# PEER feed-forward of a decode step: the seventh token block's up rows are fetched and added on VectorE instead of being multiplied on TensorE

## The chip, the cores and the metric

One NeuronCore of a Trainium2 chip. The metric is the device time of one execution in microseconds (us). The program is written directly for the five engines with semaphores; each engine runs its own list of instructions in order.

## The reference, cut to what matters

One decoder layer (convolution, window attention, memory attention, PEER feed-forward) for a prompt of 1024 tokens and 8 sample tokens, model width 1024, all in float32. The change touches only the last part, the PEER feed-forward:

```
q = (xb @ w_q).reshape(PEER_BLOCK, PEER_HEADS, 2, PEER_DK_HALF)
s = jnp.einsum('thcd,hcnd->thcn', q, keys, preferred_element_type=jnp.float32)
sv, si = lax.top_k(s, PEER_TOPK)
...
eid = i0 * PEER_N_KEYS + i1
gate = jax.nn.softmax(cv, axis=-1)
u = w_down[eid]
act = jax.nn.gelu(jnp.einsum('td,thkd->thk', xb, u, preferred_element_type=jnp.float32), approximate=False)
return jnp.einsum('thk,thkd->td', (gate * act).astype(xb.dtype), w_up[eid])
```

Every token selects 8 heads x 16 = 128 experts of 16384. For each it needs one row of `w_down` (1024 floats) for a dot product and one row of `w_up`, scaled by gate times activation, for the sum. The output is x1 plus this sum, followed by a final RMS norm.

## The kernel before, in words

The prompt is cut in 8 blocks of 128 tokens (one token on each partition). Attention and the projections run first; from about 1100 us on, the PEER part bounds the work, in three streams.

**Down rows.** For slot j of block n, GpSimd issues one indirect DMA that gathers 128 rows of `w_down`, one for each token: 512 KB (L1404, `fetch`). VectorE multiplies them with x and sums (L2019, `dot(n, j)`): 8 x 128 = 1024 such dots. Before them VectorE picks the experts (`keys`, `ids`). The rows land in a ring of SBUF slots (`rows_at`); GpSimd may fetch into a slot again once VectorE has used it. Six or seven slots are in use in the late part; one more holds the block's own x.

**Dense up.** For blocks 0 to 6 the up product is not gathered: the 128 coefficients of a token are scattered to a 128 x 128 x 128 table (VectorE builds one-hot vectors, L2043, `hot`; ScalarE scales them, L2321; TensorE multiplies them, L1469, `scatter`; ScalarE copies the table out, L2355), and TensorE multiplies this table with the whole of `w_up`. `w_up` is 128 pieces of 512 KB (L1275, `fetch_up`, on SyncE's queue, a ring of 4). The blocks are staggered by half a table: in pass n (64 pieces) TensorE multiplies each piece for block n-1 and for block n (L1666, `up_step`). So passes 0 and 7 have one block at each step ("single steps"), passes 1 to 6 two ("double steps"); passes 0 to 7 fetch 8 x 64 = 512 pieces. In the second half of pass n the table of block n+1 is scattered, one scatter at each step. When pass m+1 is over, VectorE adds block m's product to x1 (L2051, `sum`), ScalarE squares it, VectorE norms it (L2059, `norm`), SyncE writes it.

**Gathered up.** For block 7 GpSimd gathers 128 rows of `w_up` with the same ids, again 512 KB each, after the last down row, and VectorE adds each, scaled by its coefficient, to an accumulator (L2113, `up`). The adds depend on one another, so there is one semaphore wait between two.

**Sample tokens.** The 8 sample tokens' lists are made on the way. GpSimd gathers their 8 transfers of down rows (`sdown`, L1421; GpSimd first waits for the lists, which ScalarE writes and reads back after the squares of a sum), SyncE fetches 8 copies of their x rows (`scratch_xn`), VectorE makes the dots (`sdot`), GpSimd gathers 8 transfers of up rows (`sup`, L1427), TensorE sums them in the last pass ahead of step 56 (L1696), VectorE adds (`ssum`, L2095) and norms (`snorm`).

**What sets the order.** A planner (`Model`) walks through a modelled time at build and writes one list, `plan`; each engine takes its share of that list in order. So a `sum` or `ssum` stands at a fixed place among VectorE's dots, whatever the chip's real timing is: if what it waits for comes late, the dots behind it wait too.

## Time and profile before

| | us |
|---|---|
| three runs | 3344.72, 3355.07, 3366.14 |
| median of the runs | 3355.07 |
| span of the profiled execution | 3347.1 |
| busy in it: TensorE, VectorE, GpSimd | 3087.0, 2512.8, 1611.7 |
| moved by DMA in it | 1077.16 MB, 322 GB/s over the span |

The span reaches from the first to the last instruction of the profiled execution; its own time outside of the profiler is not listed, so the span stands 8.0 us under the median of the three runs. "Busy" is summed over instructions. The DMA share is the mean busy share of the 16 DMA engines; GB/s is what they moved. A "transfer" is called here what moves 512 KB (524288 bytes): one gathered row for 128 tokens, or one piece of `w_up`.

### The profile page before, as it was taken

Reading aid. Unit: us, or ns where it says so; the run is one execution under the profiler, and the core shown is the slowest. Engines: PE = TensorE matmul, PEld = TensorE weight load, DVE = VectorE, ACT = ScalarE, POOL = GpSimd, SP = SyncE. Lnnn points to the kernel's source line nnn. Section 1 sums busy time; section 2 is a strip of 40 time slices with the busy share of each in tenths; the row PEclk is TensorE's granted clock in tenths of the full one; section 3 lists DMA queues with packets and bytes.
Section 4 is the critical chain, followed back from the end, with each engine's and each line's share of the span. In section 5 each row is a group of like instructions: output and inputs, shape, how many; then the busy total and the mean of one; then the engine's idle time right before and its main releaser. Section 6 shows DMA issues by size and latency. Waiting matters only on the chain.

```text
span 3347.1 us, 33154 instructions
## 1 busy us (share of the span) xinstructions
PE 3087.0 (92%) x11349; PEld 1818.7 (54%) x11349; DVE 2512.8 (75%) x5082; ACT 779.2 (23%) x2063; POOL 1611.7 (48%) x1269
## 2 busy tenths in 40 slices
PE   8999798998989999779999999999999999997874
PEld 5677687866847654445545445545545545543321
DVE  2298434986889789888988888888888868455556
ACT  2001542321310114324214204204204214200000
POOL 0000002545145677745566667557657657444434
PEclk9999899999998999899999999999999999998998
DMA  3111466999599999999999999999999999899998
GB/s 130 43 37 58 147 204 231 336 334 354 197 339 351 359 404 397 331 368 370 381 353 388 357 380 388 344 389 385 358 377 380 359 400 373 335 410 393 408 410 316
DMA packets 326171, 1077.16 MB, mean 322 GB/s; under 512 B 40468, under 2 KB 73877, under 8 KB 325340
## 3 DMA queue, kind: packets, MB, share of 16 engines
q0 software_dynamic: 172416, 625.03, 48.7%
q1 hardware_dynamic: 119275, 428.87, 34.1%
q10 hardware_dynamic: 34312, 21.16, 2.0%
q8 instruction: 90, 1.47, 0.2%
q14 instruction: 78, 0.63, 0.1%
HBM read 1052.50 MB, written 23.94 MB: 322 GB/s over the span
## 4 chain that ended last, share of the span: by engine, by line
PE 29%; DMA 20%; DVE 15%; issue 13%; POOL 10%; ACT 1%; ACTq 1%; DVEq 0%; POOLq 0%
PE psum L1666 17%; DMA arena<-in_w_down,arena 12%; POOL arena L1404 9%; DMA arena<-in_w_up,arena 7%; DVE arena L2019 5%; PE psum L1469 4%; PE psum L1642 2%; PE psum L1529 2%; PE psum L1513 1%; ACTq L2264 1%; PE psum L1612 1%; DVE arena L2113 1%; DMA arena<-scratch_s 1%; DMA arena<-in_w_q 1%; PE psum L1515 1%
## 5 line engine op out<-in xcount | busy, mean ns | idle before, releaser
L1404 POOL DMA_INDIRECT arena<-in_w_down,arena x1024 | 1419.2, 1386 | 735.5 <-DVE arena L2019 503.1
L1666 PE MATMUL psum<-arena 128*128 128x512 f32 x3584 | 1602.0, 598 | 77.1 <-DMA arena<-in_w_up 70.8
L2019 DVE CUSTOM_DVE_ANT_0 arena<-arena 128x1024 f32<-128x1024 f32 x1024 | 1220.0, 1222 | 256.3 <-DMA arena<-in_w_down,arena 247.8
L1666 PEld LDWEIGHTS psum<-arena 128*128 128x128 f32 x3584 | 664.4, 191 | 871.0 <-issue 734.3
L1513 PE MATMUL psum<-arena 128*128 128x256 f32 (+2 forms) x1536 | 361.6, 390 | 17.0 <-DVEq L1831 5.5
L2321 ACT ACTIVATE arena<-arena 128x128 f32<-128x128 f32 x896 | 285.6, 390 | 323.8 <-DVE arena L2043 314.7
L2043 DVE TENSOR_TENSOR arena<-constants,arena 128x1024 f32<-128x1024 f32 x224 | 273.4, 1224 | 77.7 <-PE psum L1469 65.0
L1513 PEld LDWEIGHTS psum<-arena 128*128 128x128 f32 x1536 | 267.9, 195 | 99.5 <-issue 13.3
L1469 PEld LDWEIGHTS psum<-arena 128*128 128x128 f32 x1792 | 237.8, 195 | 153.2 <-ACT arena L2321 86.6
L1469 PE MATMUL psum<-arena 128*128 128x128 f32 x1792 | 245.0, 281 | 40.4 <-ACT arena L2321 40.2
L2113 DVE SCALAR_TENSOR_TENSOR arena<-arena 128x1024 f32<-128x1024 f32 x128 | 164.4, 1284 | 122.6 <-DMA arena<-in_w_up,arena 121.3
L1355 POOL DMA_DIRECT2D arena<-scratch_s x64 | 37.4, 585 | 423.5 <-DMA scratch_s<-arena 204.5
L284 PE MATMUL psum<-arena 128*128 128x344 f32 x816 | 238.4, 455 | 3.0 <-DVE arena L324 3.0
L1404 POOL DMA_INDIRECT arena<-in_w_up,arena x128 | 128.7, 1006 | 169.2 <-DVE arena L2113 150.1
L2355 ACT ACTIVATE arena<-psum 128x128 f32<-128x128 f32 (+5 forms) x512 | 149.4, 351 | 259.1 <-PE psum L1469 206.4
L284 PEld LDWEIGHTS psum<-arena 128*128 128x128 f32 x816 | 155.7, 191 | 85.3 <-issue 5.6
L1515 PE MATMUL psum<-arena 128*128 128x256 f32 (+2 forms) x768 | 183.2, 381 | 0.0
L1341 POOL MEMSET constants<- 128x64 f32 x1 | 0.2, 151 | 346.3 <-POOLq L369 346.3
L345 DVE SCALAR_TENSOR_TENSOR arena<-arena,constants 128x1024 f32<-128x1024 f32 x120 | 154.2, 1285 | 4.3
L1515 PEld LDWEIGHTS psum<-arena 128*128 128x128 f32 x768 | 132.8, 190 | 36.7
L1642 PE MATMUL psum<-arena 128*128 128x256 f32 (+2 forms) x512 | 126.1, 407 | 18.2 <-DMA arena<-in_w_q 11.3
L1529 PE MATMUL psum<-arena 128*128 128x512 f32 x256 | 119.8, 615 | 12.6 <-DVE constants L1824 5.8
(317 smaller groups left out, 2039.8 us busy)
## 6 DMA issues: line engine op xcount, KB each, us to landing
arena<-in_w_up SPq DMA_DIRECT2D x512, 512.0 KB
arena<-in_w_gates SPq DMA_DIRECT2D x96, 768.0 KB
arena<-in_w_o SPq DMA_DIRECT2D x40, 512.0 KB
arena<-in_w_q SPq DMA_DIRECT2D x32, 512.0 KB
arena<-in_w_down,arena POOLq DMA_INDIRECT x1024
arena<-in_w_chunks SPq DMA_DIRECT2D x26, 512.0 KB, 3.5
arena<-scratch_s POOLq DMA_DIRECT2D x64, 128.0 KB
scratch_s<-arena ACTq DMA_DIRECT2D x11, 512.0 KB
```

The lines of the kernel that those rows point to most:

```text
L284: mm = pe.matmul(psum[:, s + g, 0:GC], w[:, k, :], hT[:, k, g * GC:(g + 1) * GC], start=first, stop=last)
L1404: pool.indirect_dma_start(dst, None, table, bass.IndirectOffsetOnAxis(ap=idN[:, min(n, NT - 1) % 2, j:j + 1], axis=0)).then_inc(here, 16)
L1469: mm = pe.matmul(psum[:, 4 + g % 2, t * P:(t + 1) * P], pair[:, 1, t, :], pair[:, 0, t, :], start=True, stop=True)
L1513: pe.matmul(psum[:, b, 0:n], w[:, i, :], hT[:, i, cols], start=(i == 0), stop=(i == KD - 1))
L1515: mm = pe.matmul(psum[:, b + 1, 0:n], w[:, KD + c, :], branch[br][:, c, cols], start=(c == 0), stop=(c == NC - 1))
L1529: mm = pe.matmul(psum[0:tile_rows(t), bb + h, :], mergedT[:, t, i, :] if t < NT else mergedS[:, i, :], w[:, h * 512:(h + 1) * 512], start= ...
L1642: mm = pe.matmul(psum[:, b + h, 0:n], w[:, c, :], hT[:, c, cols], start=(c == 0), stop=(c == KD - 1))
L1666: mm = pe.matmul(psum[:, 2 * (m % 2) + h, :], coef_block(m, s % NKEYS), wup[s % WUPR][:, h * 512:(h + 1) * 512], start=first, stop=end)
L2019: dve.tensor_tensor_reduce(row, row, rowD[slot_of["x", n]], 1.0, 0.0, ALU.mult, ALU.add, dots[:, n % 3, j:j + 1]).then_inc(row_used, 1)
L2043: dve.tensor_tensor(hot_of(g), iota128.unsqueeze(1).unsqueeze(1).broadcast_to(full), ids[:, 0:2, BATCH * q:BATCH * (q + 1)].unsqueeze(3).b ...
L2113: dve.scalar_tensor_tensor(out=acc, in0=row, scalar=dots[:, (NT - 1) % 3, u:u + 1], in1=acc if u else x1last, op0=ALU.mult, op1=ALU.add).t ...
L2321: ins = act.activation(buf[:, 1, t, :], buf[:, 1, t, :], ACT.Copy, scale=ids[:, 2, c:c + 1])
```

## The change

`GB = 2` blocks, 6 and 7, now take the gathered way; `DENSE` falls from 7 to 6. The dense passes are 0 to 6 (pass 6 has single steps), so 64 pieces, one block's 32 scatters and one-hots, and 128 products of a piece with a table go away; 128 gathers of `w_up` rows and 128 adds come in. The ids of blocks 6 and 7 are both still held. Two accumulators stand where the one-hots were and take x1 by DMA; the slot of the last x is free for rows once its dots are over. Sample work is planned one pass earlier. The sum and norm of the last dense block no longer stand at the end of the plan but where the planner puts them.

```diff
-        DENSE = NT - 1
+        GB = 2
+        DENSE = NT - GB
...
-        for i in range(SLOTS * (NT + 1)):
+        for i in range(UPS):
...
-                free_from[s] = SLOTS * (f[1] + 1) if f[1] < NT - 1 else KEPT
+                free_from[s] = SLOTS * (f[1] + 1)
...
-        acc, x1last = at(40960, D), at(40960 + D, D)
-        y_at = [yb] * (DENSE - 1) + [rowD[slot_of["x", NT - 1]]]
-        rowS = [at(slot_at[5 if b < 4 else 7] + (b % 4) * D, D) for b in range(NB)]
-        xbc = [at(slot_at[0 if b < 4 else 2] + (b % 4) * D, D) for b in range(NB)]
-        ysm = at(slot_at[3], D)
+        accs = [at(40960 + D * i, D) for i in range(GB)]
+        rowS = [at(slot_at[2 if b < 4 else 3] + (b % 4) * D, D) for b in range(NB)]
+        xbc = [at(slot_at[4 if b < 4 else 6] + (b % 4) * D, D) for b in range(NB)]
+        ysm = at(slot_at[5], D)
...
-            if sum_next < DENSE - 1 and m.end.get(("passeded", sum_next + 1), m.now + 1) + (40.0 if sum_next == DENSE - 2 else 0.0) <= m.now:
+            if sum_next < DENSE and m.end.get(("passeded", sum_next + 1), m.now + 1) + (8.0 if sum_next == DENSE - 1 else 0.0) <= m.now:
...
-                    {"slist": (head_next % 2 == 0 or head_next // 2 % 2 == 1), "sdown": m.done("passeded", DENSE - 2), "ssum": last_put and m.done("suped", 0),
+                    {"slist": (head_next % 2 == 0 or head_next // 2 % 2 == 1), "sdown": m.done("passeded", DENSE - 2), "ssum": m.done("suped", 0),
...
-            if n_dot == NT and m.end.get(("passeded", DENSE - 2), m.now) + 20.0 > m.now:
+            if NT <= n_dot < NT + GB and (m.end.get(("passeded", DENSE - 2), m.now) + 20.0 > m.now or coefs <= n_dot - GB):
                 row = None
...
-        plan = m.plan + [(kind, DENSE - 1) for kind in ("sum", "norm")]
+        plan = m.plan
...
-                        table = w_down if n < NT else w_up
+                        table, u = (w_down, n) if n < NT else (w_up, n - GB)
                         pool.indirect_dma_start(dst, None, table, bass.IndirectOffsetOnAxis(
-                            ap=idN[:, min(n, NT - 1) % 2, j:j + 1], axis=0)).then_inc(here, 16)
+                            ap=idN[:, u % 2, j:j + 1], axis=0)).then_inc(here, 16)
...
                 def up(u):
-                    if u == 0:
-                        dve.wait_ge(coef_done, NT)
-                        dve.wait_ge(x1last_here, 16)
-                    else:
+                    g, j = u // SLOTS, u % SLOTS
+                    if j == 0:
+                        dve.wait_ge(coef_done, DENSE + g + 1)
+                        dve.wait_ge(x1last_here[g], 16)
+                    if u:
                         dve.wait_ge(up_sum, u)
                     row = row_wait(("up", u))
-                    dve.scalar_tensor_tensor(out=acc, in0=row, scalar=dots[:, (NT - 1) % 3, u:u + 1],
-                                             in1=acc if u else x1last, op0=ALU.mult, op1=ALU.add).then_inc(up_sum, 1)
+                    dve.scalar_tensor_tensor(out=accs[g], in0=row, scalar=dots[:, (DENSE + g) % 3, j:j + 1],
+                                             in1=accs[g], op0=ALU.mult, op1=ALU.add).then_inc(up_sum, 1)
```

The end of VectorE's list before. L2113 are the adds of up rows, L2118 and L2120 block 7's norm, L2095 to L2103 the sample tokens' sum and norm, L2051 to L2059 the sum and norm of block 6:

```order
L2113 SCALAR_TENSOR_TENSOR arena<-arena 128x1024 x31
L2051 TENSOR_TENSOR arena<-arena,psum 128x1024
...
L2113 SCALAR_TENSOR_TENSOR arena<-arena 128x1024 x81
L2118 RECIPROCAL constants<-constants 128x1
L2120 SCALAR_TENSOR_TENSOR arena<-arena,constants 128x1024
L2095 TENSOR_TENSOR arena<-arena,psum 8x1024
L2101 RECIPROCAL constants<-constants 8x1
L2103 SCALAR_TENSOR_TENSOR arena<-arena,constants 8x1024
L2051 TENSOR_TENSOR arena<-arena,psum 128x1024
L2057 RECIPROCAL constants<-constants 128x1
L2059 SCALAR_TENSOR_TENSOR arena<-arena,constants 128x1024
```

The same place now. The adds are L2119; L2029 makes block 7's coefficients; L2124 and L2126 norm a gathered block:

```order
L2024 ISA arena<-arena 128x1024
L2024 ISA arena 128x1
L2119 SCALAR_TENSOR_TENSOR arena<-arena 128x1024 x2
L2029 TENSOR_TENSOR arena<-arena,constants 128x128
L2119 SCALAR_TENSOR_TENSOR arena<-arena 128x1024 x129
L2124 RECIPROCAL constants<-constants 128x1
L2126 SCALAR_TENSOR_TENSOR arena<-arena,constants 128x1024
L2119 SCALAR_TENSOR_TENSOR arena<-arena 128x1024 x125
L2124 RECIPROCAL constants<-constants 128x1
L2126 SCALAR_TENSOR_TENSOR arena<-arena,constants 128x1024
```

The adds are 256 in a row with nothing else among them but two short steps, and all sums of dense blocks have moved ahead of them.

The sample tokens' sum (L2100 now) has moved among block 7's dots (L2024), on VectorE, with what each waits for:

```order
L2024 ISA arena<-arena 128x1024 [waits row2_here]
L2024 ISA arena 128x1
L2100 TENSOR_TENSOR arena<-arena,psum 8x1024 [waits sample_x1_here,sample_up]
L2024 ISA arena<-arena 128x1024 [waits row5_here]
L2024 ISA arena 128x1
```

It stands 22 dots behind the sum of block 4, with 47 dots behind it; the sum of block 5 comes 8 dots after it, with 39 behind. Before, the plan had 52 dots behind the sum of block 4, and the sample sum behind all adds.

GpSimd's gathers at the end of its list, before:

```order
L1404 DMA arena<-in_w_down,arena 128x1024 x80
L1421 DMA arena<-in_w_down,constants 128x1024 x8
L1404 DMA arena<-in_w_down,arena 128x1024 x52
L1404 DMA arena<-in_w_up,arena 128x1024 x19
L1427 DMA arena<-in_w_up,constants 128x1024 x8
L1404 DMA arena<-in_w_up,arena 128x1024 x109
```

and now (the sample tokens' down rows, L1426 now, have moved ahead of block 7's x):

```order
L1426 DMA arena<-in_w_down,constants 128x1024 x8
L1409 DMA arena<-in_w_down,arena 128x1024 x7
L1360 DMA arena<-scratch_s 128x256
...
L1409 DMA arena<-in_w_down,arena 128x1024 x18
L1403 DMA arena<-scratch_xn 128x1024
L1409 DMA arena<-in_w_down,arena 128x1024 x42
L1432 DMA arena<-in_w_up,constants 128x1024 x8
L1409 DMA arena<-in_w_down,arena 128x1024 x90
L1409 DMA arena<-in_w_up,arena 128x1024 x256
```

The 256 gathers of up rows stand as one run at the end, where there were 128.

## Rows read from the trace of the kernel before

**Rows 1.** costliest groups of the page, whole span
```profile
L1404 POOL DMA_INDIRECT arena<-in_w_down,arena x1024 | 1419.2, 1386 | 735.5 <-DVE arena L2019 503.1
L1666 PE MATMUL psum<-arena 128*128 128x512 f32 x3584 | 1602.0, 598 | 77.1 <-DMA arena<-in_w_up 70.8
L2019 DVE CUSTOM_DVE_ANT_0 arena<-arena 128x1024 f32<-128x1024 f32 x1024 | 1220.0, 1222 | 256.3 <-DMA arena<-in_w_down,arena 247.8
```

**Rows 2.** windows: busy us of each engine, TensorE clock, DMA share, GB/s
```profile
core 0: us, PE busy (x) PEld busy (x) DVE busy (x) ACT busy (x) POOL busy (x), PEclk, DMA share, GB/s
1700.00:1950.00 250.00, 244.15 (x755) 124.08 (x755) 221.47 (x505) 66.59 (x201) 159.58 (x118) 0.99 0.96 368
...
2640.60:3347.00 706.40, 611.72 (x1568) 271.51 (x1566) 442.29 (x615) 79.87 (x221) 353.10 (x305) 0.96 0.97 379
...
2850.00:2900.00 50.00, 50.00 (x171) 26.66 (x170) 29.49 (x43) 20.05 (x55) 25.41 (x18) 1.00 0.81 288
3150.00:3250.00 100.00, 74.23 (x146) 25.84 (x144) 53.87 (x44) 2.73 (x4) 38.23 (x40) 0.97 1.03 410
```

**Rows 3.** DMA view from 2640.6 us to the end
```profile
DMA packets 75523, 267.47 MB, mean 379 GB/s; under 512 B 10279, under 2 KB 10279, under 8 KB 75501
...
arena<-in_w_up SPq DMA_DIRECT2D x188, 512.0 KB
arena<-scratch_xn SPq DMA_DIRECT2D x8, 512.0 KB, 17.6
```

**Rows 4.** timeline of VectorE, the sums of blocks 3 and 4
```profile
2640.61 1.21 DVE L2051 TENSOR_TENSOR arena<-arena,psum 128x1024 f32<-128x1024 f32 x1
...
2887.05 1.22 DVE L2051 TENSOR_TENSOR arena<-arena,psum 128x1024 f32<-128x1024 f32 x1 [3.10 <-PE psum L1666]
```

**Rows 5.** timeline of TensorE, two steps in pass 5's second half
```profile
2857.45 3.60 PE L1666 MATMUL psum<-arena 128*128 128x512 f32 x8
...
2861.78 3.60 PE L1666 MATMUL psum<-arena 128*128 128x512 f32 x8
```

**Rows 6.** chain that ended last, one double step
```profile
2861.94 3.44 PE psum L1666 x8
```

**Rows 7.** timeline of GpSimd and VectorE where sample rows are fetched
```profile
2892.88 0.93 POOL L1421 DMA_INDIRECT arena<-in_w_down,constants  x1 [17.93 <-DMA constants<-scratch_gate]
...
2917.91 1.23 DVE L2019 CUSTOM_DVE_ANT_0 arena<-arena 128x1024 f32<-128x1024 f32 x1 [29.64 <-DMA arena<-in_w_down,arena]
```

**Rows 8.** timeline of TensorE, behind the sample tokens' x rows
```profile
3039.26 21.11 PE L1666 MATMUL psum<-arena 128*128 128x512 f32 x42 [17.45 <-DMA arena<-in_w_up]
```

**Rows 9.** timeline in pass 7, rows and pieces together, sample product
```profile
3269.33 1.28 DVE L2113 SCALAR_TENSOR_TENSOR arena<-arena 128x1024 f32<-128x1024 f32 x1 [1.28 <-DMA arena<-in_w_up,arena]
3269.35 1.98 PE L1666 MATMUL psum<-arena 128*128 128x512 f32 x4 [0.58 <-DMA arena<-in_w_up]
...
3271.88 1.28 DVE L2113 SCALAR_TENSOR_TENSOR arena<-arena 128x1024 f32<-128x1024 f32 x1 [1.27 <-DMA arena<-in_w_up,arena]
...
3278.94 13.90 PE L1696 MATMUL psum<-arena,constants 128*8 128x512 f32 x32
```

**Rows 10.** timeline of VectorE and GpSimd, up rows without pieces
```profile
3286.46 11.85 DVE L2113 SCALAR_TENSOR_TENSOR arena<-arena 128x1024 f32<-128x1024 f32 x9 [0.48 <-DMA arena<-in_w_up,arena]
...
3288.01 1.86 POOL L1404 DMA_INDIRECT arena<-in_w_up,arena  x1 [0.83 <-DVE arena L2113]
...
3301.18 0.94 POOL L1404 DMA_INDIRECT arena<-in_w_up,arena  x1 [0.30 <-issue]
```

**Rows 11.** windows in which hardly any piece is fetched, columns as rows 2
```profile
3293.00:3298.00 5.00, 5.00 (x12) 2.16 (x12) 4.86 (x5) 0.00 (x0) 3.88 (x4) 1.00 0.96 338
3315.00:3320.00 5.00, 0.00 (x0) 0.00 (x0) 4.72 (x4) 0.00 (x0) 3.78 (x5) 0.50 0.94 320
```

**Rows 12.** timeline of the end
```profile
3329.34 2.61 DVE L2113 SCALAR_TENSOR_TENSOR arena<-arena 128x1024 f32<-128x1024 f32 x2 [0.65 <-DMA arena<-in_w_up,arena]
...
3335.00 0.34 SPq L1332 DMA_DIRECT2D out<-arena  x1
...
3343.27 0.33 SPq L1287 DMA_DIRECT2D out<-arena  x1
```

More of the change, by code:

```diff
@@ L796, in build_kernel @@
         y_out = sem("y_out")
-        x1last_here = sem("last_x1_here")
+        x1last_here = [sem(f"last_x1_here{i}") for i in range(GB)]
         up_sum = sem("up_sum_step")
@@ L929, in ask_rows @@
                     n, j = min(i // SLOTS, NT), i % SLOTS
-                    needs = ("ids", max(n, 0), 0) if f == ("x", 0) else ("ids", n, j // TOPK) if n < NT else ("coef", NT - 1)
+                    needs = ("ids", max(n, 0), 0) if f == ("x", 0) else ("ids", n, j // TOPK) if n < NT else \
+                        ("ids", NT - 1, HEADS - 1)
                     if f[0] == "x" and n:
@@ L1052, in first_of_set @@
             return next(k for k in set_starts if u in out_set(k))
-        sevac_next, last_put = 0, False
-        while dot_next < SLOTS * (NT + 1) or not last_put or norms_due or sum_next < DENSE - 1 or sample_at < len(SAMPLE):
+        sevac_next, last_next = 0, 0
+        while dot_next < UPS or last_next < GB or norms_due or sum_next < DENSE or sample_at < len(SAMPLE):
             m.advance()
@@ L1099, in build_kernel @@
                 continue
-            if dot_next == SLOTS * (NT + 1) and not last_put and m.end["up", SLOTS - 1] + 3.0 <= m.now:
-                m.put("last")
-                last_put = True
+            if last_next < GB and m.end.get(("up", SLOTS * last_next + SLOTS - 1), m.now) + 4.0 <= m.now:
+                m.put("last", last_next)
+                last_next += 1
                 continue
@@ L1175, in build_kernel @@
                 row = max(row, x) if x is not None else None
-            if n_dot == NT and m.end.get(("passeded", DENSE - 2), m.now) + 20.0 > m.now:
+            if NT <= n_dot < NT + GB and (m.end.get(("passeded", DENSE - 2), m.now) + 20.0 > m.now or coefs <= n_dot - GB):
                 row = None
-            if row is not None and row <= m.now + 0.3 and dot_next < SLOTS * (NT + 1):
+            if row is not None and row <= m.now + 0.3 and dot_next < UPS:
                 m.now = max(m.now, row)
-                m.put(*(("dot", n_dot, dot_next % SLOTS) if n_dot < NT else ("up", dot_next % SLOTS)))
+                m.put(*(("dot", n_dot, dot_next % SLOTS) if n_dot < NT else ("up", dot_next - SLOTS * NT)))
                 m.row_done[dot_next] = m.now
@@ L1221, in rec_index @@
             return NX + recs.index(s) + 1
+        tail = [s for s in plan if s[0] in ("snorm", "last") or s in (("norm", DENSE - 2), ("norm", DENSE - 1))]
         row_order = [s for s in plan if s[0] in ("dot", "up")]
@@ L1310, in _ @@
                         sp.wait_ge(scat_done, NBATCH * DENSE)
-                        t = NT - 1
-                        sp.dma_start(x1last, scratch_x1[t * P:(t + 1) * P, :]).then_inc(x1last_here, 16)
+                        for g in range(GB):
+                            t = DENSE + g
+                            sp.dma_start(accs[g], scratch_x1[t * P:(t + 1) * P, :]).then_inc(x1last_here[g], 16)
                     if i == 38 and k == DENSE - 1:
@@ L1318, in _ @@
                         sp.dma_start(ysm[0:NB], scratch_x1[SEQ:T, :]).then_inc(xsm_here, 16)
-                    if i == 16 and k == DENSE:
-                        sp.wait_ge(row_used, SLOTS * NT)
-                        t = DENSE - 1
-                        sp.dma_start(y_at[DENSE - 1], scratch_x1[t * P:(t + 1) * P, :]).then_inc(x1_here, 16)
-                    if i == 40 and k == DENSE:
-                        write_block(DENSE - 2)
-                t = NT - 1
-                for x in plan:
+                for x in tail:
                     if x == ("snorm",):
@@ L1329, in _ @@
                         sp.dma_start(y_sample, ysm[0:NB, :]).then_inc(xsm_here, 16)
-                    elif x == ("last",):
-                        sp.wait_ge(l_ready, 1)
-                        sp.dma_start(y_prompt[t * P:(t + 1) * P, :], acc).then_inc(x1last_here, 16)
-                    elif x == ("norm", DENSE - 1):
+                    elif x[0] == "last":
+                        g = x[1]
+                        sp.wait_ge(l_ready, g + 1)
+                        t = DENSE + g
+                        sp.dma_start(y_prompt[t * P:(t + 1) * P, :], accs[g]).then_inc(x1last_here[g], 16)
+                    elif x == ("norm", DENSE - 2):
+                        write_block(DENSE - 2)
+                        fetch_x1(DENSE - 1)
+                    else:
                         write_block(DENSE - 1)
                 sp.wait_ge(y_out, 16 * DENSE)
-                sp.wait_ge(x1last_here, 32)
+                for g in range(GB):
+                    sp.wait_ge(x1last_here[g], 32)
                 sp.wait_ge(xsm_here, 32)
@@ L2058, in norm_out @@
                     dve.wait_ge(rec_done, rec_index("norm", m))
-                    dve.scalar_tensor_tensor(out=y_at[m], in0=y_at[m], scalar=mrec, in1=gfb, op0=ALU.mult,
+                    dve.scalar_tensor_tensor(out=yb, in0=yb, scalar=mrec, in1=gfb, op0=ALU.mult,
                                              op1=ALU.mult).then_inc(y_ready, 1)
```

46 lines of the change are left out of this document (25 added, 21 removed).

## The prediction

> **What bounds the kernel now.** I read the page's costliest groups first: GpSimd's gathers, TensorE's `up_step` and VectorE's dots are each around or above 1220 us, and none fills the span. TensorE's products wait 77 us in all, mostly for `w_up` pieces; GpSimd waits 503 us for VectorE to free a slot [rows 1]. The windows settle it: in the late part the DMA engines are 96 to 103% busy whatever the compute engines do (but for the list stall at 2850 us, below), at 368 to 379 GB/s in mixed stretches and 410 GB/s where only 512 KB transfers run [rows 2]. So in the part that the change touches the bound is transfers: one takes 524288 bytes / 410 GB/s = 1.28 us.
>
> The last stretch shows it best. In pass 7 each add on VectorE waits 1.27 us for its row, each single step on TensorE waits for its piece, and both start every 2.55 us: two transfers of 1.28 us, taken in turns [rows 9]. Neither engine is the limit: a single step's work is half a double step's 3.44 us, 1.72 us [rows 6], an add is 1.28 us.
>
> **The change in bytes.** I count from 2640.6 us, where the sum of block 3 starts [rows 4]; up to there the two plans are the same but for the sample gathers. From there the kernel before moves 267.47 MB in 706.4 us, 188 pieces among them [rows 2, 3]. Removed: 64 pieces. Added: 128 gathered rows. Net 64 transfers or 33.6 MB: 301.0 MB, which at 410 GB/s is 734 us, where 267.5 MB would be 652 us. Before therefore has 706 - 652 = 54 us of unused DMA time in the stretch. Even if all of it went but the end behind the last landing (8 us, below), the span would be 2640.6 + 734 + 8 = 3383 us, 36 us above the 3347.1 us now. That is the floor.
>
> **What comes out, and its cover.** 64 single steps (64 x 1.72 = 110 us of TensorE) and 32 scatters. In pass 5's second half a step takes 4.33 us with its scatter and 3.44 us of that is the product [rows 5, 6], so 32 x 0.89 = 28 us goes there; 32 one-hots leave VectorE. Little of this sets the end, since both engines wait for transfers behind it. It only brings pass 6 forward.
>
> **Pass 5 after the change.** 64 x 3.44 = 220 us. The sample tokens' 8 x-row transfers on SyncE's queue now fall into this pass; before, TensorE waited 17.5 us behind them [rows 8]. Pass 5 ends at 2640.6 + 220 + 17 = 2878 us (before, the sum behind it starts at 2887 [rows 4]). In these 237 us the DMA engines could make 185 transfers. GpSimd's stall for the sample lists (17.9 us; VectorE then waits 29.6 us [rows 7]) moves here from pass 6; in its window 288 GB/s instead of 410 are moved [rows 2], 50 x 122 / 410 = 15 us lost, 12 transfers. Minus 64 pieces, 8 x rows, 16 sample rows and 2 blocks of x1, 83 dots are fed. The plan has 95 ahead of the sum of block 4: VectorE comes some 12 dots late, and TensorE does not wait for it.
>
> **Pass 6 after.** Single steps and rows in turns, 2.56 us for a pair [rows 9]. VectorE has 12 + 22 = 34 dots to do before the sample sum: 87 us, TensorE is then at step 34. Now comes the new wait: the sample sum stands at a fixed place ahead of 47 dots and needs TensorE's product ahead of step 56. VectorE stops; GpSimd fills the ring (7 rows and 7 pieces, 18 us) and stops too; TensorE makes the last 15 steps at 1.72 us (26 us) and the product (14 us [rows 9]). 145 us into the pass VectorE goes on; the last 8 steps take 17 us (4 pieces have landed, 4 share). Pass 6 ends 162 us in, at 3040 us. Idle DMA time of the stall: 15 x 0.44 + some 9 = 16 us.
>
> **Rows alone.** Of the 164 dots behind 2640.6 us 83 + 34 + 7 + 4 = 128 rows are fetched by then; 36 remain, and 256 up rows: 292 with no pieces beside them. What this runs at is the largest unknown, since before always has pieces there but for two short stretches. VectorE alone can take a row in 11.85 / 9 = 1.32 us, from rows that had landed [rows 10]. GpSimd's ten issues of the same stretch are nine intervals in 13.17 us, 1.46 us each [rows 10]. The DMA engines moved 338 and 320 GB/s in such windows, 1.55 to 1.64 us a row, though 94 to 96% busy [rows 11]; some of that is a ring that was just run empty. I take 1.46 us, in the middle and from the longest row, and keep 1.32 and 1.60 as ends. 292 x 1.46 = 426 us, to 3466 us.
>
> The Trainium skill (DMA: Bandwidth & Descriptors, Issuing engines are not separate DMA queues) says that DMAs started from different engines share the same 16 DMA engines and that starting them from several saves only issue time. By that rule rows alone would move as fast as rows and pieces together; the windows above disagree so far. It is the first rival below.
>
> **The end.** From the last row's landing: an add, square, root, reciprocal, norm, output. Before, the last add starts at 3329.34 + 1.31 and block 7's output is issued at 3335.00; the last output is issued at 3343.27 and the span ends 3.8 us later [rows 12]. The gathered block is now the last, the sample's and block 6's norms no longer follow it: 1.3 + 3.1 + 3.8 = 8 us, and 8.3 us are saved. Sum by steps: 3466 + 8 = 3474 us.
>
> **The same by bytes.** 734 + 8 (end) + 15 (list stall) + 16 (sample sum) + 292 x 0.18 = 53 (rows alone above 1.28) = 826 us, 3467 us. I take 3470 us of span, 123 us above 3347.1. The median of the runs is 8.0 us above the span, so 3355.07 + 123 = 3478 us.
>
> **The rivals.**
> 1. *Rows alone run at VectorE's pace.* For it: the nine adds at 1.32 us [rows 10]. Against: VectorE was emptying a full ring. Time: 292 x 0.14 = 41 us less, 3437; if the sample sum is not late either, 16 us less again, 3421.
> 2. *Rows alone run slower still,* at 1.60 us, because the DMA engines do not move more with one queue: 292 x 0.14 more, 3519. For it the two windows, against it their shortness.
> 3. *The floor.* All idle time goes: 3383 + 8 = 3391, just outside 1%. It needs rows alone at 1.28 us, which nothing reached.
> 4. *Faster: the DMA bound is only apparent* and transfers follow the computing engines, as they do in pass 5's second half, where VectorE and TensorE go in lock-step at 2 dots a step. Then TensorE's 110 + 28 us fall away and VectorE is the chain: from 2640.6 us 164 dots at 1.22, 256 adds at 1.32 and some 40 us of other work are 578 us, span 3219, time 3227. It decides if the DMA engines can move 301 MB in 578 us, 521 GB/s; the windows stop at 410 [rows 2]. I exclude that the change does not do what it says: the order shows 256 adds, and 448 pieces are left.
>
> **How the numbers follow.** Forecast as worked out: 0.55 (3450 to 3505). Rival 1: 0.2. Rival 2: 0.15. Floor or a little better: 0.04. Faster: 0.02. Something longer than any of these, such as a further wait of VectorE at the moved sums: 0.04. The range reaches from rival 1 without the late sum to rival 2: 3420 to 3520. This kernel's measurement can tell about 1% (34 us) from no change, so "same" is up to 3389: 0.04. Faster 0.02, slower 0.94.
>
> **What the profile after would show.** GB/s near 410 with both queues until pass 6 is over near 3040 us, then one long run of L2119 with GpSimd's gathers at 1.3 to 1.6 us and TensorE idle, at 330 to 395 GB/s. The sum of block 4 near 2880. VectorE waiting some 50 us at L2100 for TensorE. 64 pieces fewer in SyncE's issues, 1110 MB in all. The output issued 3 us behind the last add. I would be wrong if TensorE's idle tail were much shorter than 400 us, or if GB/s rose above 410 anywhere.

## The result, and the profile after

| | before | after |
|---|---|---|
| median of the runs, us | 3350.68 (4 runs) | 3467.31 (4 runs) |
| lowest to highest | 3344.72 to 3366.14 | 3463.67 to 3477.61 |
| span of the profiled execution | 3347.1 | 3475.8 |

The changed kernel is slower: 1.0354 times the time before, 95% interval 1.0317 to 1.0392. The forecast was 3478 us, in 3420 to 3520. The profiled execution is the longest of the four: its own time is 3477.61 us, 1.8 us over its span. Part of its length comes from ahead of the change: the sum of block 3 starts at 2646.79 us, where before it starts at 2640.61 [rows 4], and in the experiments below, all with the same work up to there, it starts anywhere from 2634 to 2651. So I also give, for every run, the time **from the sum of block 3 to the end of the span**: 706.5 us before, 829.0 us after, 122.5 more. Spans are read that way wherever a few microseconds matter.

The page of the changed kernel, costliest groups, as in [rows 1]. A row gives the count of the instructions, then the engine's busy time in them and the mean length of one in ns, then the engine's idle time just before them and what ended most of it:

```profile
L1409 POOL DMA_INDIRECT arena<-in_w_down,arena x1024 | 1391.2, 1359 | 844.1 <-DVE arena L2024 617.4
...
L1671 PE MATMUL psum<-arena 128*128 128x512 f32 x3072 | 1371.0, 598 | 58.0 <-DMA arena<-in_w_up 54.2
...
L2119 DVE SCALAR_TENSOR_TENSOR arena<-arena 128x1024 f32<-128x1024 f32 x256 | 328.9, 1285 | 28.3 <-DMA arena<-in_w_up,arena 19.2
...
L1409 POOL DMA_INDIRECT arena<-in_w_up,arena x256 | 279.9, 1093 | 78.9 <-issue 77.4
```

TensorE has 231 us less of `up_step` and the time is longer. The last row is where to look: 256 gathers of up rows, with nothing to wait for that the profile shows (77.4 of the 78.9 us of idle time are "issue"). Each is 1.093 us long on average, with 0.30 us ahead of it.

Windows of the changed kernel (columns as in [rows 2]; the third reaches from pass 5 to the moment at which VectorE is held up by nothing else, and the last two hold rows alone):

```profile
2640.00:2880.00 240.00, 223.91 (x531) 99.88 (x530) 134.29 (x302) 8.72 (x14) 113.34 (x104) 0.96 0.98 381
...
3000.00:3050.00 50.00, 42.33 (x97) 14.29 (x95) 11.89 (x19) 1.44 (x3) 10.68 (x8) 1.00 0.66 240
...
2640.00:3053.00 413.00, 362.12 (x825) 148.81 (x823) 195.45 (x399) 12.89 (x21) 160.93 (x150) 0.98 0.95 367
3100.00:3200.00 100.00, 0.00 (x0) 0.00 (x0) 89.35 (x80) 0.31 (x1) 78.67 (x71) 0.50 0.97 365
3310.00:3400.00 90.00, 0.00 (x0) 0.00 (x0) 87.56 (x69) 0.00 (x0) 69.58 (x68) 0.50 1.02 402
```

The hole is at 3000 us, 240 GB/s, and its cause stands in VectorE's waits from 2640 us to the end (total, times, longest):

```profile
DVE arena L2024 <- DMA arena<-in_w_down,arena: 159.4, 104, 29.7
DVE arena L2100 <- PE psum L1701: 53.6, 1, 53.6
DVE arena L2119 <- DMA arena<-in_w_up,arena: 19.2, 47, 1.1
DVE arena L2056 <- DMA arena<-scratch_x: 10.4, 1, 10.4
```

The second line is the forecast wait of the sample sum. The fourth was not forecast: block 5's sum waits 10.4 us for its x1, which SyncE fetches only behind its 448th piece and once block 4's write is over. On the timeline of VectorE (and the end):

```profile
3027.63 1.21 DVE L2100 TENSOR_TENSOR arena<-arena,psum 8x1024 f32<-8x1024 f32 x1 [53.58 <-PE psum L1701]
...
3053.07 1.22 DVE L2056 TENSOR_TENSOR arena<-arena,psum 128x1024 f32<-128x1024 f32 x1 [10.36 <-DMA arena<-scratch_x]
...
3465.29 3.92 DVE L2119 SCALAR_TENSOR_TENSOR arena<-arena 128x1024 f32<-128x1024 f32 x3 [0.18 <-DMA arena<-in_w_up,arena]
...
3472.27 0.33 SPq L1333 DMA_DIRECT2D out<-arena  x1
```

At 3053 us 39 dots and 256 adds are left, 295 rows. The last add ends at 3469.2: 416.2 us, **1.41 us a row**.

Two regimes of that stretch, timeline of GpSimd and VectorE. In the first the gathers differ in length, here from 1.01 to 1.52 us; in the second, from about 3312 to 3433 us, they are all 1.01 to 1.02 us long. Behind 3433 us the first is back:

```profile
3226.20 1.01 POOL L1409 DMA_INDIRECT arena<-in_w_up,arena  x1 [0.30 <-issue]
...
3227.51 1.52 POOL L1409 DMA_INDIRECT arena<-in_w_up,arena  x1 [0.30 <-issue]
3229.34 1.11 POOL L1409 DMA_INDIRECT arena<-in_w_up,arena  x1 [0.30 <-issue]
...
3230.76 1.14 POOL L1409 DMA_INDIRECT arena<-in_w_up,arena  x1 [0.30 <-issue]
...
3232.20 1.32 POOL L1409 DMA_INDIRECT arena<-in_w_up,arena  x1 [0.30 <-issue]
...
3343.77 9.21 DVE L2119 SCALAR_TENSOR_TENSOR arena<-arena 128x1024 f32<-128x1024 f32 x7
3344.85 1.01 POOL L1409 DMA_INDIRECT arena<-in_w_up,arena  x1 [0.30 <-issue]
3346.17 1.02 POOL L1409 DMA_INDIRECT arena<-in_w_up,arena  x1 [0.30 <-issue]
```

In the second regime starts 1.32 us apart are 1.02 + 0.30; VectorE makes seven adds in 9.21 us, 1.32 each. So three things lie close together there (VectorE's add, GpSimd's gather, a transfer at 1.28 us), and the experiments had to take them apart.

### The profile page after: what moved, and what is told of

Read it like the earlier page. It is cut to its first block, busy times and chain, and to the rows that moved or that the text cites. A ratio compares the mean times of both kernels' runs of the same rounds, so it can differ in the third digit from the quotient of the medians.

```text
span 3475.8 us, 31673 instructions
## 1 busy us (share of the span) xinstructions
PE 2830.5 (81%) x10578; PEld 1692.0 (49%) x10578; DVE 2639.9 (76%) x5177; ACT 717.7 (21%) x1871; POOL 1735.2 (50%) x1397
## 3 DMA queue, kind: packets, MB, share of 16 engines
q8 instruction: 84, 1.38, 0.2%
## 4 chain that ended last, share of the span: by engine, by line
PE 28%; DVE 17%; DMA 17%; POOL 13%; issue 13%; ACT 1%; ACTq 1%; SPq 0%; DVEq 0%; POOLq 0%
PE psum L1671 18%; POOL arena L1409 13%; DMA arena<-in_w_down,arena 9%; DVE arena L2024 5%; DVE arena L2119 4%; PE psum L1474 3%; DMA arena<-in_w_up 3%; PE psum L1647 1%; PE psum L1534 1%; PE psum L1518 1%; DMA scratch_s<-arena 1%; DVE arena L2048 1%; ACTq L2270 1%; DMA arena<-scratch_s 1%; PE psum L1520 1%
## 5 line engine op out<-in xcount | busy, mean ns | idle before, releaser
L1409 POOL DMA_INDIRECT arena<-in_w_down,arena x1024 | 1391.2, 1359 | 844.1 <-DVE arena L2024 617.4
L2024 DVE CUSTOM_DVE_ANT_0 arena<-arena 128x1024 f32<-128x1024 f32 x1024 | 1221.8, 1222 | 317.2 <-DMA arena<-in_w_down,arena 311.6
L1671 PE MATMUL psum<-arena 128*128 128x512 f32 x3072 | 1371.0, 598 | 58.0 <-DMA arena<-in_w_up 54.2
L1671 PEld LDWEIGHTS psum<-arena 128*128 128x128 f32 x3072 | 569.7, 191 | 739.5 <-issue 627.2
L2119 DVE SCALAR_TENSOR_TENSOR arena<-arena 128x1024 f32<-128x1024 f32 x256 | 328.9, 1285 | 28.3 <-DMA arena<-in_w_up,arena 19.2
L1518 PEld LDWEIGHTS psum<-arena 128*128 128x128 f32 x1536 | 269.5, 196 | 110.2 <-issue 13.3
L1409 POOL DMA_INDIRECT arena<-in_w_up,arena x256 | 279.9, 1093 | 78.9 <-issue 77.4
L2327 ACT ACTIVATE arena<-arena 128x128 f32<-128x128 f32 x768 | 244.7, 390 | 316.5 <-DVE arena L2048 316.5
L2048 DVE TENSOR_TENSOR arena<-constants,arena 128x1024 f32<-128x1024 f32 x192 | 233.9, 1222 | 54.6 <-PE psum L1474 54.4
L1474 PEld LDWEIGHTS psum<-arena 128*128 128x128 f32 x1536 | 205.0, 196 | 138.7 <-ACT arena L2327 75.5
L1474 PE MATMUL psum<-arena 128*128 128x128 f32 x1536 | 211.6, 282 | 42.3 <-ACT arena L2327 42.0
L284 PEld LDWEIGHTS psum<-arena 128*128 128x128 f32 x816 | 155.6, 191 | 85.3 <-issue 5.4
L2361 ACT ACTIVATE arena<-psum 128x128 f32<-128x128 f32 (+2 forms) x448 | 128.2, 346 | 191.0 <-PE psum L1474 190.0
L1520 PEld LDWEIGHTS psum<-arena 128*128 128x128 f32 x768 | 132.8, 190 | 36.7
L1534 PE MATMUL psum<-arena 128*128 128x512 f32 x256 | 118.6, 610 | 19.8 <-DVE constants L1829 9.9
```

What stands on the lines that cost most here:

```text
L284: mm = pe.matmul(psum[:, s + g, 0:GC], w[:, k, :], hT[:, k, g * GC:(g + 1) * GC], start=first, stop=last)
L1409: pool.indirect_dma_start(dst, None, table, bass.IndirectOffsetOnAxis(ap=idN[:, u % 2, j:j + 1], axis=0)).then_inc(here, 16)
L1474: mm = pe.matmul(psum[:, 4 + g % 2, t * P:(t + 1) * P], pair[:, 1, t, :], pair[:, 0, t, :], start=True, stop=True)
L1518: pe.matmul(psum[:, b, 0:n], w[:, i, :], hT[:, i, cols], start=(i == 0), stop=(i == KD - 1))
L1520: mm = pe.matmul(psum[:, b + 1, 0:n], w[:, KD + c, :], branch[br][:, c, cols], start=(c == 0), stop=(c == NC - 1))
L1671: mm = pe.matmul(psum[:, 2 * (m % 2) + h, :], coef_block(m, s % NKEYS), wup[s % WUPR][:, h * 512:(h + 1) * 512], start=first, stop=end)
```

## The experiments

Those with half rows or half adds give other values for the two gathered blocks, or omit a block, as each expectation says. "Pace" is the time between the first and the last of the 256 gathers of up rows, over 255: 1.402 us in the changed kernel (3104.2 to 3461.7). Paces, lengths of gathers and times from block 3's sum come from one profiled execution of each kernel, and the kernels did not all run on one chip, so a difference of 10 us in them is a hint and no more.

### 1. The moved sums: late_sums

```diff
-        plan = m.plan
+        plan = list(m.plan)
+        for what, before in ((("ssum",), ("up", 24)), (("snorm",), ("up", 29)),
+                             (("sum", DENSE - 1), ("up", 33)), (("norm", DENSE - 1), ("up", 41))):
+            plan.remove(what)
+            plan.insert(plan.index(before), what)
```

> The changed kernel with four steps of the plan moved: the sample tokens' sum and norm and the sum and norm of block 5 stand behind the first 24 to 41 adds of up rows instead of among block 7's dots. My theory: VectorE's 53.6 us wait for the sample product and its 10.4 us wait for x1 cost what the DMA engines leave unused meanwhile, 20 to 33 us (240 GB/s in 50 us and 314 GB/s in the next 50, against 410). Time 20 to 33 us below the changed kernel's 3467, no wait over 5 us on VectorE at these steps, and GB/s at 400 or more until pass 6 is over. Rival A: VectorE is the chain from there to the end, so the whole 64 us come back, 3403. Rival B: the wait is hidden, since the dots behind it would have waited for their rows anyway: no change.

Measured: 3427.53 us (3419.36 to 3433.86), 1.0213 of before [1.0185, 1.0241], 40 us under the changed kernel; from the sum of block 3 on 783.0 us, 46 less. Both waits are gone, and the window up to 3053 us, which read 367 GB/s, reads:

```profile
2640.00:3053.00 413.00, 359.72 (x798) 143.57 (x796) 223.89 (x425) 11.41 (x15) 189.13 (x180) 0.98 1.01 396
```

At 3053 us 265 rows are left and not 295, but late_sums starts the stretch 6.65 us earlier. Counted from block 3's sum, GpSimd has 299 gathers left in the changed kernel and 298 in late_sums 324 us on, where VectorE is about to stop in the one, and 289 against 262 at 406.2 us (3053.0 and 3046.35). 27 gathers at 1.41 us are 38 us: that is what the two waits cost, more than my 20 to 33 us. The other 8 of the 46 us are the gathers that follow, 1.38 us apart in place of 1.41.

### 2. What paces rows alone: half_rows, half_adds, half_both

```diff
+                        if n >= NT:
+                            dst, table = dst[:, 0:D // 2], table.rearrange("e (a n) -> (e a) n", a=2)
```
```diff
-                    dve.scalar_tensor_tensor(out=accs[g], in0=row, scalar=dots[:, (DENSE + g) % 3, j:j + 1],
-                                             in1=accs[g], op0=ALU.mult, op1=ALU.add).then_inc(up_sum, 1)
+                    dve.scalar_tensor_tensor(out=accs[g][:, 0:512], in0=row[:, 0:512], scalar=dots[:, (DENSE + g) % 3, j:j + 1],
+                                             in1=accs[g][:, 0:512], op0=ALU.mult, op1=ALU.add).then_inc(up_sum, 1)
```

The first is half_rows, the second half_adds, both together half_both.

> The changed kernel with each gathered up row cut to half: 512 of 1024 columns (256 KB a transfer), read from half the address, so that other values arrive; adds and issues are as they were. If the DMA engines pace the stretch in which rows run alone (1.40 us a row on the mean, 364 GB/s in its first 250 us), the adds come every 1.32 us throughout and the time is some 15 to 25 us less. If GpSimd's issue or VectorE's adds pace it, the time stays within 8 us. A fall to 0.7 us a row would show that neither limits, which I exclude: both take 1.32 us.

> The changed kernel with each add of an up row done on 512 of 1024 columns (the other half of these two blocks' sum is left out); all rows are fetched whole. Adds take 0.7 us instead of 1.28. If VectorE paces the rows that run alone, GpSimd at 1.24 to 1.32 us and the DMA engines at 1.28 come next and the time falls by 20 us or more. If the DMA engines or GpSimd's issue pace it, VectorE waits for every row and the time is the same within 8 us.

> Half rows and half adds together (both as in the two kernels before). Only GpSimd's issue of 128 descriptors is left at its full size. If it is a pace of its own at 1.32 us (1.02 and 0.30), the time is that of the half rows alone within 5 us; if VectorE's add slows the issue, an issue takes 0.94 us and the pace is 1.24 us, 256 x 0.08 = 20 us less than the half rows alone; if GpSimd is no limit, far less.

| | time of the one execution, us | from block 3's sum | pace, us | DMA 3200 to 3300, GB/s |
|---|---|---|---|---|
| changed kernel | 3477.61 | 829.0 | 1.402 | 364 |
| half_rows | 3455.55 | 820.0 | 1.328 | 204 |
| half_adds | 3466.42 | 818.0 | 1.323 | 407 |
| half_both | 3481.43 | 831.5 | 1.418 | 184 |

By my own conditions neither of the first two runs is clear: half_rows is 9 us shorter from block 3's sum (15 to 25 would have spoken for the transfers, under 8 for GpSimd or VectorE), half_adds 11 us (20 or more would have spoken for VectorE). The paces say more. With half the bytes the rows come every 1.33 us (half_rows, VectorE 97% busy), which is VectorE's add; but a gather of 1.018 us and the 0.30 us ahead of it make 1.32 us too, so this run alone does not tell the two apart. psum_sums in section 3 does. With half the add (752 ns) they come every 1.28 us in the steady part around 3250 us. Windows of half_adds:

```profile
3200.00:3300.00 100.00, 0.00 (x0) 0.00 (x0) 58.60 (x79) 2.73 (x4) 74.00 (x77) 0.50 1.02 407
```

GpSimd's queue alone moves 407 GB/s, as much as two queues do in pass 7 [rows 2]. So the low windows of before [rows 11] were not a limit of one queue. Nor does a DMA share near 1 prove that transfers are the bound: the changed kernel shows 0.97 at 365 GB/s, half_adds 1.02 at 407. The Trainium skill (DMA: Bandwidth & Descriptors, Issuing engines are not separate DMA queues) says that DMAs from all engines share the same 16 DMA engines and a second issuing engine saves only issue time; this run agrees with it.

The surprise is half_both: half the bytes and half the add, and it is the slowest, 26 us above half_rows, which none of my three cases had. Its groups from 3100 to 3400 us:

```profile
L1411 POOL DMA_INDIRECT arena<-in_w_up,arena x208 | 230.9, 1110 | 63.4 <-issue 62.2 <-DVE arena L2121 1.2
L2121 DVE SCALAR_TENSOR_TENSOR arena<-arena 128x512 f32<-128x512 f32 x205 | 154.2, 752 | 132.1 <-DMA arena<-in_w_up,arena 129.0 <-issue 1.7 <-DVE arena L2121 1.2
```

VectorE waits for rows, the DMA engines are 65 to 69% busy, and the gather is 1.110 us long, 0.17 us more than the 0.94 us it takes at its shortest. So the gather's own length sets the pace, and it is not fixed.

### 3. Why the gather gets longer: sums in PSUM

An add reads the row and the accumulator, both in SBUF. Here the accumulators stand in PSUM, so that each add but the first of a block has one input in SBUF and not two, and each but the last writes PSUM. The row lands where it did. late_psum_sums has the move of experiment 1 as well; psum_half_both and psum_half_adds are the PSUM forms of half_both and half_adds.

```diff
+        psum_at = [psum[:, 4:6, :], psum[:, 0:2, :]]
...
-                    dve.scalar_tensor_tensor(out=accs[g], in0=row, scalar=dots[:, (DENSE + g) % 3, j:j + 1],
-                                             in1=accs[g], op0=ALU.mult, op1=ALU.add).then_inc(up_sum, 1)
+                    sum_at = psum_at[g] if j < SLOTS - 1 else halves(accs[g])
+                    dve.scalar_tensor_tensor(out=sum_at, in0=halves(row), scalar=dots[:, (DENSE + g) % 3, j:j + 1],
+                                             in1=psum_at[g] if j else halves(accs[g]), op0=ALU.mult,
+                                             op1=ALU.add).then_inc(up_sum, 1)
```

> The changed kernel with the running sums of its two gathered blocks in TensorE's result memory (PSUM): an add reads the fetched rows from SBUF and the sum from PSUM, and writes PSUM; only the last add of a block writes SBUF. Everything else stands as it was, the number of gathers and adds too. Theory A: GpSimd's gather (1.02 to 1.17 us in the runs so far, 1.09 mean in the changed kernel) is stretched because VectorE's add takes both its inputs from SBUF beside it. Then the mean gather falls to 0.94 to 1.0 us, a row in the stretch without pieces costs 1.25 to 1.30 us in place of 1.41, 295 rows save 30 to 47 us, and the time is 3420 to 3437 us. The Trainium skill, SBUF — State Buffer, section on who interferes with whom, says that VectorE operations with two SBUF inputs and GpSimd shut each other out of a shared port, and ones with at most one SBUF input do not; it also says that this does not hold for the making of DMA descriptors, and by that sentence nothing changes. Theory B: the gather's length is its own and the queue's; then nothing moves, 3460 to 3475 us. Theory C: an add with PSUM on both sides takes longer than the 1.285 us of now; at 1.45 us VectorE would pace the rows and the time would be 3480 us or more.

> The same sums in PSUM together with the move of late_sums (the sample sum, its norm, block 5's sum and norm further back among the adds). late_sums took 3427 us with 265 rows after the pieces at 1.37 us. Theory A: 265 rows at 1.25 to 1.30 us, 19 to 32 us less, 3395 to 3408 us, still above the kernel before at 3350. Theory B: 3422 to 3434 us. Theory C: slower than late_sums, by 20 us at an add of 1.45 us.

> half_both (the gathered up rows of 256 KB, each add on 512 of its 1024 columns; other values come out, the number of instructions stays) with the running sum in PSUM. In half_both neither the DMA engines (67% busy) nor VectorE (55%) was full, and the gather itself set the pace: 1.110 us long on average, a row every 1.41 us. Theory A, VectorE's operations with two SBUF inputs lengthen the gather: the mean gather falls to 0.94 to 0.96 us and a row comes every 1.24 to 1.27 us, 290 rows save some 43 us, span 3428 to 3440 us. Theory B, in psum_sums the gather was only shorter because VectorE set a steady beat: mean gather 1.05 us or more, a row every 1.36 us or more, span 3465 to 3485 us.

> half_adds (full rows of 512 KB, adds on 512 of 1024 columns, so other values) with the running sum in PSUM. VectorE is out of the way and so, by theory A, is the lengthening of the gather (0.976 us in half_adds between 3100 and 3400 us). Then the transfers set the pace throughout: 1.28 us a row at 405 to 410 GB/s from the end of the pieces to the end, and the span is 3440 to 3450 us, where half_adds had 3465.8. If the late part of half_adds (1.40 us a row beyond 3415 us) came from the DMA engines, nothing moves.

| sums in SBUF, then PSUM | mean gather after 3053 us | pace, us | from block 3's sum |
|---|---|---|---|
| half_both, psum_half_both | 1.113, 0.951 | 1.418, 1.257 | 831.5, 791.4 |
| half_adds, psum_half_adds | 0.990, 0.943 | 1.323, 1.299 | 818.0, 802.9 |
| changed kernel, psum_sums | 1.093, 0.945 | 1.402, 1.332 | 829.0, 820.2 |
| late_sums, late_psum_sums | 1.057, 0.953 | 1.370, 1.349 | 783.0, 780.2 |

The first line decides. Groups of psum_half_both from 3100 to 3400 us, against those of half_both above:

```profile
L1415 POOL DMA_INDIRECT arena<-in_w_up,arena x239 | 227.4, 951 | 73.2 <-issue 58.5 <-DVE psum L2126 14.0 <-DVE arena L2030 0.7
L2126 DVE SCALAR_TENSOR_TENSOR psum<-arena,psum 128x512 f32<-128x512 f32 x234 | 176.7, 755 | 113.4 <-DMA arena<-in_w_up,arena 113.0
```

The add is as long as before (755 and 752 ns) and only its second input and its output moved; the gather is 0.16 us shorter and the stretch 40 us. Theory A had 43. The two ran on different chips, but that is not the cause: the 123 gathers of down rows between 2640 and 3000 us, for which nothing was changed, are 1.056 us long on average in half_both and 1.073 in psum_half_both. Input and output moved together, so which of the two accesses of SBUF lengthens the gather stays open. In psum_half_adds the gather is short as well and the transfers set the pace, at 402 to 409 GB/s; its end was expected at 3440 to 3450 us of span and came at 3451.2.

The Trainium skill (SBUF — State Buffer, Who interferes with whom) says that a VectorE instruction with at most one SBUF input, outside certain modes, does not contend with GpSimd, and the means of 0.943 to 0.953 us agree. It says that one with two SBUF inputs contends with a GpSimd instruction that reads SBUF, not with one that only writes it, and it infers, for `tensor_tensor`, that the making of descriptors is left alone, since that needs the write side. 1.113 against 0.951 us show that the gather is lengthened. They do not refute the inference: the gather also reads its 128 row numbers from SBUF (`idN`), and the add's output was moved with its input. Whether that reading, the making of descriptors or the add's write is behind it was not tried.

For the changed kernel itself the cure brought little: psum_sums takes 3464.23 us (3462.31 to 3472.33), 1.0338 of before [1.0313, 1.0363], which is not to be told from 1.0354 [1.0317, 1.0392], and late_psum_sums 3429.56 us, 1.0246 [1.0217, 1.0274], beside late_sums' 1.0213 [1.0185, 1.0241]. My expectation of 1.25 to 1.30 us a row was wrong by its own numbers: VectorE's add with PSUM is 1.290 us, and one follows another after 0.03 us, so 1.32 us is what VectorE allows. Groups of psum_sums from 3100 to 3400 us:

```profile
L2124 DVE SCALAR_TENSOR_TENSOR psum<-arena,psum 128x1024 f32<-128x1024 f32 x208 | 268.3, 1290 | 8.0 <-DMA arena<-in_w_up,arena 0.9
L1413 POOL DMA_INDIRECT arena<-in_w_up,arena x217 | 205.2, 946 | 83.9 <-issue 75.4 <-DVE psum L2124 7.0 <-DVE arena L2028 1.2
```

So rows alone have three floors close together: VectorE 1.32 us, the transfers 1.28 to 1.30, GpSimd 1.25 if nothing lengthens its gather and 1.42 if something does.

### 4. The price of the block, and the bound of before: no_block6_up, half_pieces

no_block6_up is the changed kernel without block 6's gathers and adds (its output is left out, it is not multiplied either); half_pieces is the kernel before with pass 7's pieces cut to half their columns:

```diff
-                        table, u = (w_down, n) if n < NT else (w_up, n - GB)
+                        table, u = (w_down, n) if n < NT else (w_up, NT - 1)
```
```diff
-                    sp.dma_start(wup[s % WUPR], w_up[e * NKEYS:(e + 1) * NKEYS, :])\
+                    cols = slice(0, D if s < HALF * DENSE else D // 2)
+                    sp.dma_start(wup[s % WUPR][:, cols], w_up[e * NKEYS:(e + 1) * NKEYS, cols])\
```

> Only the removing half of the change: block 6 is neither multiplied nor gathered (its up product and its output are left out; block 7 is gathered as in both kernels). Against the kernel before this takes out 64 pieces, 128 products and 32 scatters and adds nothing. My theory, transfers bound the stretch: 64 x 1.28 = 82 us less DMA work, of which some is lost again to the sample sum's wait and to rows alone: 50 to 75 us below the kernel before, and the changed kernel is 128 x 1.32 to 1.45 = 170 to 185 us above it. Rival: TensorE and scatters set the time before, then 110 + 28 = 138 us less than before.

> The kernel before with the 64 pieces of w_up in pass 7 fetched by half (512 of 1024 columns, the other half of a table piece is what an older piece left, so block 6's product is wrong in half its columns); every instruction of the compute engines is as before. If transfers bound the tail, 64 x 0.64 = 41 us less (33 to 42). If the transfers only follow the engines, no change.

no_block6_up: 3293.27 us (3276.3 to 3299.24), 0.9818 [0.9791, 0.9846]. Taking block 6's up product out of TensorE and giving it to nobody is worth 56 us (3349.2 in those runs of before); giving it to GpSimd and VectorE costs 174 us, 1.36 us for each of 128 rows (176.5 us and 1.38 counted from block 3's sum). Both stalls stand in its trace too.

half_pieces: 3310.4 us (3306.02 to 3312.93), 0.9874 [0.9858, 0.9891], 39 us less, where 64 halves of a transfer, 0.64 us each, are 41. Its window in pass 7:

```profile
3150.00:3250.00 100.00, 89.77 (x183) 31.59 (x182) 68.19 (x54) 0.90 (x2) 49.31 (x53) 0.98 1.03 402
```

402 GB/s, nearly what whole pieces give (410), with 54 operations on VectorE where there were 44 [rows 2]: the tail of the kernel before is bound by transfers, and fewer bytes turn into more rows at once.

### 5. A version that beats both: tuned_before

The experiments say that the block should stay on TensorE and the stalls should go. In the kernel before these are GpSimd's wait for the sample lists at 2850 us [rows 7] and the sums behind the last add [rows 12]:

```diff
-        plan = m.plan + [(kind, DENSE - 1) for kind in ("sum", "norm")]
+        plan = list(m.plan)
+        plan.remove(("sdown",))
+        plan.insert(plan.index(("dot", NT - 1, 88)), ("sdown",))
+        for what in (("ssum",), ("snorm",)):
+            plan.remove(what)
+        for what, before in ((("ssum",), 112), (("snorm",), 117), (("sum", DENSE - 1), 119), (("norm", DENSE - 1), 124)):
+            plan.insert(plan.index(("up", before)), what)
```

> The kernel before with plan steps moved only: GpSimd's gather of the sample tokens' down rows 13 dots later (it is queued ahead of row fetches and waits 17.9 us for the lists, in a window in which 288 instead of 410 GB/s are moved), and the sample tokens' sum and norm and block 6's sum and norm among the last 16 adds instead of behind them. My theory: up to 15 us and 8 us less, 10 to 23 us in all, 0.3 to 0.7%. Rival: the steps among the last adds delay the adds by as much as they save at the end, and the later gather delays the sample product: no change.

3335.36 us (3324.9 to 3344.86, 6 runs), 0.9946 of before [0.9924, 0.9967]: 14 us less, and 692.6 us from the sum of block 3 on in place of 706.5. The window of the list wait, 288 GB/s before [rows 2], reads

```profile
2850.00:2900.00 50.00, 50.00 (x184) 27.70 (x183) 39.37 (x56) 22.21 (x67) 36.35 (x24) 1.00 0.99 366
```

and the last output is issued 3.1 us behind the last add. A gain of half a per cent, from order alone; it is less than the 1% that I had held this measurement able to tell, though the interval leaves 1 out. The two moves were not tried one by one.

## Why the prediction was right

**The bound.** Transfers in the part that the change touches: held, by half_pieces (39 us measured, 41 by bytes) and by the pairs of row and piece, still 2.56 us apart in pass 6. Rival 4, that the DMA bound is only apparent, is out: from 1100 us on no 50 us of any of these traces moved more than 414 GB/s, and it needed 521. Of the rows alone it does not hold: there the gather's length sets the pace for most of the way, and the DMA share of 0.97 that goes with it is no bound.

**Passes 5 and 6.** The forecast is on the clock of before, and the profiled run starts the stretch 6.2 us later. Moved by that, it had VectorE stop at 2971 us, go on at 3029 and pass 6 end at 3046; the trace has 2974 (3027.63 less 53.58), 3028, and TensorE's last step ending at 3046.0. These steps were right within 3 us. The wait for the sample lists moved to pass 5 as said (VectorE waits 29.7 us). "The sum of block 4 near 2880" was wrong, and against the working ahead of it: with VectorE 12 dots late at 2.56 us a dot it comes 31 us behind the end of pass 5, and the trace has it at 2917.66 us.

**The stall's price was the mis-sized term.** "Idle DMA time of the stall" was 16 us; removing both waits gave 40 us in the medians and 46 from block 3's sum, 38 of them by the waits themselves. The first 406.2 us from block 3's sum read 371 GB/s in the changed kernel and 396 in late_sums, and 406 x 25 / 410 = 25 us of transfers, where I had counted 16 and had left out the fetch of block 5's x1 and the 10.4 us of waiting for it. The rest is that the stall had to be priced in gathers and not in bytes. From VectorE's stop to 3053 us GpSimd starts ten of them, late_sums in the same time 36, and each of the 27 that the changed kernel is behind is paid for later at 1.41 us, not at 1.28. Why late_sums' gathers are shorter (1.057 against 1.093 us) was not tried by itself; its trace has more stretches of the even regime.

**Rows alone.** Forecast 292 rows at 1.46 us, 426 us from 3040 us on; measured 295 at 1.41, 416.2 us from 3053 on. The value was near, the reason given ("in the middle and from the longest row") was none. The row itself [rows 10] mixes two things, as the trace between its ends shows: of the nine intervals seven are 1.32 us, and two are longer because their gathers are.

```profile
3288.01 1.86 POOL L1404 DMA_INDIRECT arena<-in_w_up,arena  x1 [0.83 <-DVE arena L2113]
3290.18 1.02 POOL L1404 DMA_INDIRECT arena<-in_w_up,arena  x1 [0.30 <-issue]
3291.50 1.01 POOL L1404 DMA_INDIRECT arena<-in_w_up,arena  x1 [0.30 <-issue]
...
3299.43 1.45 POOL L1404 DMA_INDIRECT arena<-in_w_up,arena  x1 [0.30 <-issue]
```

These are the two regimes of the stretch after. So 1.46 us was near 1.41 by luck: nothing in the prediction says how often either would occur.

half_both and its PSUM form show what is behind the long ones: the gather, 0.94 us by itself, is lengthened beside VectorE's adds if their sum is in SBUF. Rival 1 (1.32 us, VectorE's pace) is what one sees in the changed kernel from 3312 to 3433 us and throughout psum_sums; rival 2 (one queue moves less) is refuted by half_adds. The floor of 1.28 us, "which nothing reached", was reached only with half adds.

**The sum.** 3040 + 426 + 8 = 3474 forecast; 3053 + 416.2 + 6.6 = 3475.8 measured. 13 us too little ahead of the rows alone (6 of them the late start of this execution) and 10 too much in them met. Two errors of opposite sign nearly cancel, and that is luck. The output is issued 3.1 us behind the last add, as said. I added 8.0 us for what lies outside of the span; it is 1.8 us, so the profiled execution of before was some 6 us shorter than the median of its three runs. The forecast of 3478 is 11 us above the median of the changed kernel, in part by that.

## What to carry to other kernels

A block moved from an engine that shares a stream (64 pieces for one block in a single-step pass) to one that fetches its own (128 rows) must be priced in bytes first; here it also left 295 rows for the end, where nothing else is left for the DMA engines and each row costs a gather (1.41 us on average) and not its bytes (1.28 us). When software-issued gathers pace a stretch, look at the spread of their length beside VectorE's operations, and try a running sum in PSUM if the gather is the longest of the steps; it brought 40 us in half_both and nearly nothing in the changed kernel, where VectorE's own 1.32 us came next. A sum that is put at a fixed place in an engine's list should be moved back until what it needs is certainly there: that was worth about 40 us here, without another instruction.

## What the runs showed that I had not expected

- A gather of 128 rows is 0.94 to 0.95 us on average with 0.30 us ahead of it if the running sum of VectorE's adds is in PSUM, and 0.99 to 1.11 us if it is in SBUF; single ones of 1.8 us and more stand in traces of either kind. With the sum in SBUF it depends on how the two fall together, and half_adds has three cases in one trace: an add that starts 0.26 us behind the gather leaves it at 0.94 us, one at 0.69 us makes it 0.98, and one at 0.93 us, close to its end, 1.09 to 1.11.

```profile
3243.70 0.94 POOL L1409 DMA_INDIRECT arena<-in_w_up,arena  x1 [0.35 <-issue]
3243.96 0.75 DVE L2119 SCALAR_TENSOR_TENSOR arena<-arena 128x512 f32<-128x512 f32 x1 [0.53 <-issue]
...
3164.21 0.98 POOL L1409 DMA_INDIRECT arena<-in_w_up,arena  x1 [0.30 <-issue]
3164.90 0.75 DVE L2119 SCALAR_TENSOR_TENSOR arena<-arena 128x512 f32<-128x512 f32 x1 [0.53 <-issue]
...
3388.64 1.11 POOL L1409 DMA_INDIRECT arena<-in_w_up,arena  x1 [0.30 <-issue]
3389.58 0.75 DVE L2119 SCALAR_TENSOR_TENSOR arena<-arena 128x512 f32<-128x512 f32 x1 [0.64 <-DVE arena L2119]
```

- Taking half of the bytes and half of VectorE's work away left the stretch as long as it was (831.5 us, 829.0 in the changed kernel), while either alone is a little shorter (820.0 and 818.0). In half_both three of four gathers have the next add start 0.8 to 1.2 us behind them, the costly place in half_adds. That VectorE's or the transfers' steady beat keeps gathers and adds out of it in the other two, and nothing does with both halved, is argued from the timelines and was not tried by itself.
- 402 to 409 GB/s from GpSimd's queue alone.
- The same work up to the sum of block 3 took 2634 to 2651 us in the profiled executions, so a span has some 17 us of scatter that the change has no part in. They ran on several chips, and how much of it is between chips was not tried.
